# Two memory heads' scores inside the inversion, two weight splits and two PSUM banks moved, in the first mixer of a hybrid-layer chain

## The chip, the cores and the metric

One core of one Trainium2 chip. The metric is the device time of the whole kernel in microseconds (us); lower is better. 0.3% of it, 3.8 us, is about what a measurement of this kernel can tell from no change.

## The reference

The kernel computes a first hybrid layer (pooling and forgetting attention over 272 tokens of width 1024) and then two layers with feed-forward blocks of width 2816. The change lies in the mixer of the first of these two layers, which adds a gated delta rule (6 heads of 128, two chunks of 128 tokens here) and an attention over 256 memory rows (4 heads of 64):

```python
h = rms_norm(x, mix_norm) @ a_w_in               # 26 columns of 128: k, q, v, q_mem, gate
qkv = silu(causal_depthwise_conv(qkv, conv_w))
t_mat = where(strict, (k_beta k^T) * decay, 0) + eye      # one per head, inverted
u, w = inv(t_mat) (v * beta), inv(t_mat) (k_beta * exp(g))
# recurrence over the chunks
v_new = u_c - w_c state
out   = q_c state + qk_c v_new
state = state * d_c + k_c^T v_new
# memory attention, 4 heads
o_m = softmax(q_mem k_mem^T / 8) v_mem
x = x + concatenate([rms_norm(o) * silu(gate), o_m]) @ w_out
```

## The kernel before

All matrices that come from weights are streamed: SyncE loads slabs of two units (a unit is one column of 8 blocks of 128x128) into a ring of 4 (`raw`), ScalarE rounds a unit into `w_hi`, VectorE writes the rest into `w_lo`, and TensorE does three products for each block, so that the sum has float32 accuracy. On ScalarE `slot(u)` is the rounding of unit u+4, on VectorE `slot(u)` is the low half of unit u+3. TensorE waits for the low half of its unit (`unit_begin`), and SyncE's next load into a slab waits for it as well. Every engine's order of work is written out by hand; engines wait on counting semaphores only.

**The input projection of the mixer** is a loop over t = 0 to 24 on each engine (`for t in range(26)` on ScalarE and VectorE, `for t in range(25)` on TensorE), one unit of `w_in_a` for each t. Beside it run, for each tile, the convolution taps on VectorE (L1383), Silu on ScalarE (L764), and in the last turns the preparation of the delta rule: TensorE's Gram products of head h at t = 17 + h (L2232), GpSimd's differences of decays, ScalarE's two Exp of them for each head (L801, L802), and VectorE's `grams(h)` at t = 18 + h (L1357, L1359), which joins both and counts `n_ready`. The Gram product of head h waits for `n_ready` of head h - 2 (for h = 3 to 5), because they share banks. At t = 13 ScalarE takes the Exp of a few columns (L788, L789). At t = 19, 21 and 23 TensorE turns two heads' values (L2244) into a side bank, and ScalarE scales them back to SBUF at t = 20, 22 and 24 (L812, `vt_done`); the second turn waits for the first `vt_done`.

**The inversion** has 7 levels in two groups of three heads. In each of the first 6 levels TensorE does, for each group, a product (L2170 on `side`) and three transposes (L2165), and then for each group a joining product (L2170 on `main`). VectorE masks between them (`first_factor` L1373, `second_factor` L1377), ScalarE copies (`copy_packed` L818, `inv_x` L825), GpSimd masks the next level's factor (L1836). The groups' factors lie in main banks 3 and 0, `product` in side banks 0 and 2, `turn_bank` in side banks 3 and 1.

**The recurrence** (`each`, L2293) follows. With E1 to E6 for its six rounds of six heads, S0 to S3 for a memory head's scores (L1919), P0 to P3 for the four transposes of its probabilities (L1935), O0 to O3 for its outputs (L1961), and T for the last six transposes of the inversion (L2165), TensorE's order is:

```
S0 E1 T S1 P0 E2 E3 S2 E4 O0 P1 S3 E5 O1 P2 E6 O2 P3 O3, squares of the outputs (L2338)
```

A memory head also needs VectorE's `row_maxima` (L1042, L1058) after S, ScalarE's `exps` (L555, two instructions) after that, VectorE's `normalise` (L1066, L1068) before P, and ScalarE's `copy_pt` (L564) between P and O. E1 writes the new values that ScalarE copies (`new_values`, L830); E2 (which waits for both groups' last `second_factor`) makes the new state, E3 and E6 make outputs that VectorE copies (`by_heads`, L1486) and ScalarE squares (L836, L838), E4 prepares the second chunk's right-hand side (L1505), E5 its new values. VectorE's low halves (L986 into `w_lo`) stand between these, `slot(u0 + 24)` behind the copies of E3 and `slot(u0 + 25)` behind the last `normalise`; ScalarE's `slot(u0 + 25)` (L519) stands behind the copies of E1. `scores(MEM_A)` and `scores(MEM_A + 1)` write to side banks 0 and 3, and E1 writes to main banks 1 and 2. Then the outputs are normed and gated (L1519 to L1541, with two table loads on ScalarE, L861 and L865), and `mix_out` multiplies them by `w_out`.

Of the kernel before, what the change touches and what calls it, by code (L numbers as in the profile page):

```python
# [14 lines left out]
P = 128  # L15
# [133 lines left out]
def program(nc, dram, out):  # L149
    with ExitStack() as ctx:  # L150
# [180 lines left out]
        evac = sem("evac")  # L331
# [89 lines left out]
        def gram_bank(h):  # L421
            return (side[3], side[1], side[0])[h % 3]
# [4 lines left out]
        def product(g):  # L427
            return side[2 * g]
# [19 lines left out]
        def score_bank(a):  # L448

            return side[3] if a >= MEM_A and a % 2 else side[0]  # L450
# [51 lines left out]
        def _(act):  # L502
# [249 lines left out]
            for t in range(26):  # L752
# [46 lines left out]
                for h in {18: (0,), 19: (1, 2), 20: (3,), 21: (4, 5)}.get(t, ()):  # L799
                    act.wait_ge(diff_ready, h + 1)  # L800
                    act.activation(dec[:, h, 0, :], dec[:, h, 0, :], ACT.Exp, scale=-1.0)  # L801
                    act.activation(dec[:, h, 1, :], dec[:, h, 1, :], ACT.Exp).then_inc(decay_ready, 1)  # L802
                    if h == 3:
                        act.wait_ge(diff_ready, DH)
                        act.activation(spread[:, :, P:SEQ], spread[:, :, P:SEQ], ACT.Exp).then_inc(late_ready, 1)
                if t in (20, 22, 24):
                    j = (t - 20) // 2
                    act.wait_ge(turned_v, j + 1)
                    act.wait_ge(kv_ready, 1)
                    for i in range(4):  # L810
                        h, c = 2 * j + i // 2, i % 2
                        ins = act.activation(kqv[:, 12 + h, c * P:(c + 1) * P], side[2][:, i * P:(i + 1) * P],  # L812
                                             ACT.Copy, scale=kv_scale[:, c, h:h + 1])
                    ins.then_inc(vt_done, 1)
# [5 lines left out]
            for level in range(1, LEVELS):  # L820
                for g in range(GROUPS):
                    copy_packed(g, level)
                for g in range(GROUPS):
                    act.wait_ge(x_ready, 2 * level - 1 + g)
                    act.activation(inv_x[:, g, :, :], by_three(product(g)), ACT.Copy).then_inc(x_copied, 1)  # L825
            for g in range(GROUPS):
                copy_packed(g, LEVELS)
            def new_values(dst, j, seen):
                act.wait_ge(rec_pe, seen)
                act.activation(dst[:, 3 * j:3 * j + 3, :], rec[j][:, 0:3 * P], ACT.Copy).then_inc(rec_act, 1)  # L830
# [10 lines left out]
            exps(MEM_A)  # L841
            new_values(vn0, 0, 1)
            new_values(vn0, 1, 2)
            slot(u0 + 25)
            exps(MEM_A + 1)
            copy_pt(MEM_A)
            act.wait_ge(rec_dve, 4)
            square_outputs(0)
            exps(MEM_A + 2)
            copy_pt(MEM_A + 1)  # L850
            new_values(vn1, 0, 9)
# [123 lines left out]
        def _(dve):  # L975
# [498 lines left out]
            for level in range(1, LEVELS):  # L1474
                if level > 1:
                    for g in range(GROUPS):
                        first_factor(g, level)
                for g in range(GROUPS):
                    second_factor(g, level, turn_bank(g))
            for g in range(GROUPS):  # L1480
                first_factor(g, LEVELS)
# [7 lines left out]
            dve.wait_ge(q_decayed, 1)  # L1489
            row_maxima(MEM_A)  # L1490
            for g in range(GROUPS):
                second_factor(g, LEVELS, packed(g))
            row_maxima(MEM_A + 1)
            normalise(MEM_A)
            for j in range(2):
                by_heads(state, rec[2 + j], j, 3 + j)
            normalise(MEM_A + 1)
            for j in range(2):
                by_heads(o_a[:, :, 0:P], rec[j], j, 5 + j)
            slot(u0 + 24)  # L1500
            row_maxima(MEM_A + 2)
# [7 lines left out]
            row_maxima(MEM_A + 3)  # L1509
            take_output(om_a[:, 0, :], MEM_A + 1)  # L1510
# [346 lines left out]
        def _(pe):  # L1857
# [322 lines left out]
            for t in range(25):  # L2180
# [37 lines left out]
                if t >= 17 and t - 17 < DH:  # L2218

                    h = t - 17  # L2220
                    bank = gram_bank(h)
                    if h == 0:
                        pe.wait_ge(sums_ready, 1)
                    elif h == 1:
                        pe.wait_ge(kt_done, 1)
                    elif h == 2:
                        pe.wait_ge(sums_ready, 2)
                    else:
                        pe.wait_ge(n_ready, h - 2)
                    for i, other in enumerate((h, 6 + h)):  # L2230
                        for c in range(2):
                            ins = pe.matmul(bank[:, (2 * i + c) * P:(2 * i + c + 1) * P], kqv[:, h, chunks[c]],  # L2232
                                            kqv[:, other, chunks[c]], start=True, stop=True)
                    ins.then_inc(gram, 1)
                if t in (19, 21, 23):
# [3 lines left out]
                    if j == 0:  # L2239
                        pe.wait_ge(kt_done, 2)  # L2240
                    else:
                        pe.wait_ge(vt_done, j)
                    for i in range(4):
                        ins = pe.transpose(side[2][:, i * P:(i + 1) * P],  # L2244
# [24 lines left out]
            for level in range(1, LEVELS):  # L2269
# [8 lines left out]
                for g in range(GROUPS):  # L2278
# [3 lines left out]
                        .then_inc(joined, 1)  # L2282

# [12 lines left out]
            scores(MEM_A)  # L2296

            pe.wait_ge(evac, in_tile(25) + 1)
            each(rec[0:2], [(lambda h: d_t[:, h, 0, :], lambda h: kqv[:, 12 + h, 0:P])],
                 (((first_ready, 2 * LEVELS - 1),), ((first_ready, 2 * LEVELS),)))  # L2300
            for g in range(GROUPS):
                pe.wait_ge(f_copied, 2 * LEVELS - 1 + g)
                turn(g, lambda i: inv_f[:, i // 3, i % 3, :], packed(g))
            scores(MEM_A + 1)
# [4 lines left out]
                 (((rec_act, 1),), ((rec_act, 2),)))  # L2309

            each(rec[0:2], [(lambda h: vn0[:, h, :], lambda h: a_t[:, 2 * h, :])], ((), ()))
            scores(MEM_A + 2)
# [3 lines left out]
            outputs(MEM_A)  # L2316
            turn_probs(MEM_A + 1)
            scores(MEM_A + 3)

            each(rec[0:2], [(lambda h: d_t[:, h, 1, :], lambda h: rhs1[:, h, :])],  # L2320
                 (((rec_dve, 7),), ((rec_dve, 10),)))
            outputs(MEM_A + 1)
# [370 lines left out]
```

## Time and profile before

| | |
|---|---|
| Median of 3 runs | 1263.31 us (1261.05 to 1264.09) |
| The profiled execution: its time | 1260.43 us |
| The profiled execution: its span | 1258.4 us |
| Mean granted TensorE clock | 0.993 of full speed |
| TensorE busy | 1224.1 us, 97% of the span |
| VectorE busy | 872.0 us, 69% |
| ScalarE busy | 689.5 us, 55% |
| GpSimd busy | 97.3 us, 8% |

The span is counted from the first to the last instruction; the execution's own time is 2.0 us more, for what lies around it. A time in the rows below is in us from the start of the span. TensorE is called PE, VectorE DVE, ScalarE ACT, GpSimd POOL and SyncE SP there; "PE side L2170 x6" is a merged stretch of six pieces on a side bank (a float32 product of 128x128 shows as two). A part in square brackets is the idle time before an instruction and what ended it. Busy TensorE time is not TensorE at its peak: an instruction's time holds its latency.

### The profile page before, as it was taken

The page shows a single profiled execution, that of the slowest core. Times are in us where ns is not written, and L with a number is a line of the kernel's source. Part 1 is how long each engine was busy: PE and PEld are TensorE (multiplying, and loading weights), DVE is VectorE, ACT ScalarE, POOL GpSimd, SP SyncE. Part 2 cuts the span into 40 slices and gives each one's busy share as a digit, 9 for nine tenths or more (in the row PEclk, how much of TensorE's full clock was granted, in tenths as well). Part 3 has the DMA queues.
Part 4 walks back from the last instruction along what each step waited for, and adds up shares of the span by engine and source line. Part 5 has one row for each costly group of instructions (what it writes and reads, how often), then busy time and mean ns, then how long its engine had stood idle before and what let it go on. Part 6 is the DMA issues. An engine that isn't in the chain of part 4 may idle for free.

```text
span 1258.4 us, 25772 instructions
## 1 busy us (share of the span) xinstructions
PE 1224.1 (97%) x9976; PEld 1201.3 (95%) x9976; DVE 872.0 (69%) x1430; ACT 689.5 (55%) x1027; POOL 97.3 (8%) x106
## 2 busy tenths in 40 slices
PE   7999999999999998989999999999999999999996
PEld 6899999999999998969999999999999989999996
DVE  7576699876655888657766756866665777766653
ACT  7455466665544677455756544644444556544431
POOL 7261000000000014400000000000000010000000
PEclk9999999999999999998999999999999999999998
DMA  8434445655654444103554653555564323555621
GB/s 342 179 135 170 174 167 171 209 196 175 230 209 142 147 160 151 35 34 125 177 191 176 249 185 108 193 184 183 211 226 144 133 95 113 191 197 183 259 93 33
DMA packets 48983, 210.01 MB, mean 167 GB/s; under 512 B 3446, under 2 KB 6020, under 8 KB 44436
## 3 DMA queue, kind: packets, MB, share of 16 engines
q1 hardware_dynamic: 47424, 204.42, 46.2%
q10 hardware_dynamic: 1492, 4.68, 1.0%
q8 instruction: 44, 0.72, 0.2%
q14 instruction: 23, 0.19, 0.0%
HBM read 207.99 MB, written 1.10 MB: 166 GB/s over the span
## 4 chain that ended last, share of the span: by engine, by line
PE 92%; DVE 5%; ACT 1%; DMA 1%; issue 1%; DVEq 0%; ACTq 0%
PE main L1866 27%; PE main L1868 27%; PE main L1867 27%; DVE w_lo L986 1%; PE side L1961 1%; PE main L2170 1%; DVE cy L1383 1%; PE main L2293 1%; PE side L1935 1%; PE side L2170 1%; PE main L2445 1%; PE main L2449 1%; PE main L2447 1%; DMA spread<-delta_rows 0%; PE side L1972 0%
## 5 line engine op out<-in xcount | busy, mean ns | idle before, releaser
L519 ACT ACTIVATE w_hi<-raw 128x1024 fp32r<-128x1024 f32 (+2 forms) x364 | 404.6, 1114 | 309.3 <-PE main L1868 302.8
L1866 PE MATMUL main<-xg_hi,w_hi 128*128 128x256 f32 (+1 forms) x2000 | 566.8, 283 | 1.2 <-DVE w_lo L986 0.8
L1867 PE MATMUL main<-xg_hi,w_lo 128*128 128x256 f32 (+1 forms) x2000 | 563.6, 282 | 0.0
L1868 PE MATMUL main<-xg_lo,w_hi 128*128 128x256 f32 (+1 forms) x2000 | 563.3, 282 | 0.0
L986 DVE TENSOR_TENSOR w_lo<-raw,w_hi 128x1024 fp32r<-128x1024 f32 (+2 forms) x364 | 468.3, 1295 | 7.0 <-ACT w_hi L519 6.2
L1866 PEld LDWEIGHTS main<-xg_hi,w_hi 128*128 128x128 f32 x2000 | 378.1, 189 | 3.0 <-DVE w_lo L986 1.2
L1868 PEld LDWEIGHTS main<-xg_lo,w_hi 128*128 128x128 f32 x2000 | 378.8, 189 | 0.0
L1867 PEld LDWEIGHTS main<-xg_hi,w_lo 128*128 128x128 f32 x2000 | 376.0, 188 | 0.5
L1866 PE MATMUL main<-h_hi,w_hi 128*128 128x256 f32 x704 | 198.3, 282 | 0.0
L1868 PE MATMUL main<-h_lo,w_hi 128*128 128x256 f32 x704 | 198.3, 282 | 0.0
L1867 PE MATMUL main<-h_hi,w_lo 128*128 128x256 f32 x704 | 198.2, 282 | 0.0
L1866 PEld LDWEIGHTS main<-h_hi,w_hi 128*128 128x128 f32 x704 | 132.6, 188 | 0.0
L1867 PEld LDWEIGHTS main<-h_hi,w_lo 128*128 128x128 f32 x704 | 132.6, 188 | 0.0
L1868 PEld LDWEIGHTS main<-h_lo,w_hi 128*128 128x128 f32 x704 | 132.6, 188 | 0.0
L1108 DVE TENSOR_TENSOR hid<-main,rstd 128x256 f32<-128x256 f32 x88 | 37.3, 424 | 100.1 <-PE main L1868 100.1
L537 ACT ACTIVATE xg_hi<-x,par 128x256 fp32r<-128x256 f32 (+2 forms) x56 | 28.1, 509 | 102.7 <-DVE x L1262 91.9
L1262 DVE SCALAR_TENSOR_TENSOR x<-main,x 128x256 f32 (+1 forms) x40 | 17.0, 425 | 94.0 <-PE main L1868 94.0
L1108 DVE TENSOR_TENSOR gate_n<-main,rstd 128x256 f32<-128x256 f32 x88 | 37.3, 424 | 35.5 <-PE main L1868 34.9
L1020 DVE SCALAR_TENSOR_TENSOR xg_lo<-x,par,xg_hi 128x256 fp32r<-128x256 f32 (+2 forms) x56 | 27.2, 493 | 30.9 <-ACT xg_hi L537 30.9
L533 ACT ACTIVATE sq<-x 128x256 f32<-128x256 f32 (+2 forms) x64 | 26.1, 407 | 40.6 <-DVE x L1262 31.2
L1297 DVE TENSOR_TENSOR hid<-hid,gate_s 128x256 f32<-128x256 f32 x86 | 36.6, 426 | 7.2 <-ACT gate_s L707 0.9
L986 DVE TENSOR_TENSOR h_lo<-hid,h_hi 128x256 f32 (+1 forms) x88 | 36.9, 420 | 0.6 <-ACT h_hi L712 0.6
(420 smaller groups left out, 1421.7 us busy)
## 6 DMA issues: line engine op xcount, KB each, us to landing
raw<-in_w_gu_a SPq DMA_DIRECT2D x44, 1024.0 KB, 5.2
raw<-in_w_gu_b SPq DMA_DIRECT2D x44, 1024.0 KB, 5.2
raw<-in_w_down_a SPq DMA_DIRECT2D x16, 1408.0 KB, 5.9
raw<-in_w_down_b SPq DMA_DIRECT2D x16, 1408.0 KB, 5.9
raw<-in_w_in SPq DMA_DIRECT2D x20, 1024.0 KB, 5.3
raw<-in_w_in_a SPq DMA_DIRECT2D x13, 1024.0 KB, 5.2
raw<-in_w_up SPq DMA_DIRECT2D x4, 1024.0 KB, 5.2
raw<-in_w_out SPq DMA_DIRECT2D x4, 1024.0 KB, 5.2
```

The lines of the kernel that those rows point to most:

```text
L519: act.activation(w_hi[:, u % RING, 0:n], raw[:, s % RAW, u % 2, 0:n], ACT.Copy).then_inc(hi_ready, 1)
L533: act.activation(sq[:, c % 2, 0:n], src, ACT.Square).then_inc(sq_ready, 1)
L537: act.activation(dst, src, ACT.Copy, scale=g).then_inc(xh_ready, 1)
L986: return dve.tensor_tensor(dst, src, hi.bitcast(F32), ALU.subtract)
L1020: dve.scalar_tensor_tensor(dst, src, g, hi.bitcast(F32), ALU.mult, ALU.subtract)\
L1108: return dve.tensor_tensor(dst, main[t % 4][0:rows, c:c + n], scale, ALU.mult)
L1262: dve.scalar_tensor_tensor(xm, main[(t + m) % 4][:, 0:SEQ], alpha, xm, ALU.mult, ALU.add).then_inc(evac, 1)
L1297: dve.tensor_tensor(hid[:, t % 2, :], hid[:, t % 2, :], gate_s[:, t % 2, :], ALU.mult)\
L1866: pe.matmul(dst, a_hi, b_hi, start=first, stop=False)
L1867: pe.matmul(dst, a_lo, b_hi, start=False, stop=False)
L1868: return pe.matmul(dst, a_hi, b_lo, start=False, stop=last)
L2170: ins = pe.matmul(dst[:, i * P:(i + 1) * P], lhs(i), rhs(i), start=first, stop=True, skip_group_check=not first)
```

## The change

- TensorE: S0 (`scores(MEM_A)`) moves to the end of level 4 of the inversion and S1 to the end of level 5; both now write to main banks 1 and 2 (`rec[0]`, `rec[1]`). E1, which writes to the same banks, now waits for both heads' Exp (`exp_ready`). S2 moves between E2 and E3, O0 between E3 and E4, P1 behind E4, O1 ahead of E5.
- VectorE: the maxima of S0 move behind the second factors of level 5 and those of S1 behind those of level 6, ahead of the last `first_factor`; `normalise` of the first head stands ahead of the last `second_factor`, that of the second behind it. `slot(u0 + 24)` moves from behind the copies of E3 to behind the last maxima.
- ScalarE: `exps` of the first head moves behind the copies of level 6, that of the second behind the last `copy_packed`; `slot(u0 + 25)` moves behind `copy_pt` of the second head; `exps` of the third comes behind `copy_pt` of the first.
- Banks: the Gram products of heads 2 and 5 go to side bank 2 instead of 0, the turned values to side bank 0 instead of 2, `product` of the two groups is swapped. So the Gram product of head 2 waits for `kt_done` (ScalarE's k_dec, L796) and no longer for `sums_ready` 2 (VectorE, L1449); the first turn of values waits for `sums_ready` 2.
- ScalarE's Exp of the decays: head 0 at t = 13 (was 18), head 1 at 18, heads 2 and 3 at 19, heads 4 and 5 at 20; the Exp of `spread` (L805) follows head 5 instead of head 3, still ahead of L812 at t = 20.

```diff
         def gram_bank(h):
-            return (side[3], side[1], side[0])[h % 3]
+            return (side[3], side[1], side[2])[h % 3]
...
         def product(g):
-            return side[2 * g]
+            return side[2 - 2 * g]
...
         def score_bank(a):
+            if a in (MEM_A, MEM_A + 1):
+                return rec[a - MEM_A]
             return side[3] if a >= MEM_A and a % 2 else side[0]
...
-                for h in {18: (0,), 19: (1, 2), 20: (3,), 21: (4, 5)}.get(t, ()):
+                for h in {13: (0,), 18: (1,), 19: (2, 3), 20: (4, 5)}.get(t, ()):
...
-                    if h == 3:
+                    if h == 5:
                         act.wait_ge(diff_ready, DH)
...
-                        ins = act.activation(kqv[:, 12 + h, c * P:(c + 1) * P], side[2][:, i * P:(i + 1) * P],
+                        ins = act.activation(kqv[:, 12 + h, c * P:(c + 1) * P], side[0][:, i * P:(i + 1) * P],
...
+            exps(MEM_A)
             for g in range(GROUPS):
                 copy_packed(g, LEVELS)
+            exps(MEM_A + 1)
...
-            exps(MEM_A)
             new_values(vn0, 0, 1)
             new_values(vn0, 1, 2)
-            slot(u0 + 25)
-            exps(MEM_A + 1)
             copy_pt(MEM_A)
+            exps(MEM_A + 2)
             act.wait_ge(rec_dve, 4)
             square_outputs(0)
-            exps(MEM_A + 2)
             copy_pt(MEM_A + 1)
+            slot(u0 + 25)
             new_values(vn1, 0, 9)
...
                     second_factor(g, level, turn_bank(g))
+                if level == 5:
+                    dve.wait_ge(q_decayed, 1)
+                    row_maxima(MEM_A)
+                if level == 6:
+                    row_maxima(MEM_A + 1)
             for g in range(GROUPS):
                 first_factor(g, LEVELS)
...
-            dve.wait_ge(q_decayed, 1)
-            row_maxima(MEM_A)
+            normalise(MEM_A)
             for g in range(GROUPS):
                 second_factor(g, LEVELS, packed(g))
-            row_maxima(MEM_A + 1)
-            normalise(MEM_A)
+            normalise(MEM_A + 1)
             for j in range(2):
                 by_heads(state, rec[2 + j], j, 3 + j)
-            normalise(MEM_A + 1)
+            row_maxima(MEM_A + 2)
             for j in range(2):
                 by_heads(o_a[:, :, 0:P], rec[j], j, 5 + j)
-            slot(u0 + 24)
-            row_maxima(MEM_A + 2)
...
             row_maxima(MEM_A + 3)
+            slot(u0 + 24)
             take_output(om_a[:, 0, :], MEM_A + 1)
...
                     elif h == 2:
-                        pe.wait_ge(sums_ready, 2)
+                        pe.wait_ge(kt_done, 2)
...
                     if j == 0:
-                        pe.wait_ge(kt_done, 2)
+                        pe.wait_ge(sums_ready, 2)
...
-                        ins = pe.transpose(side[2][:, i * P:(i + 1) * P],
+                        ins = pe.transpose(side[0][:, i * P:(i + 1) * P],
...
+                if level == 4:
+                    scores(MEM_A)
+                if level == 5:
+                    pe.wait_ge(evac, in_tile(25) + 1)
+                    scores(MEM_A + 1)
...
-            scores(MEM_A)
-
-            pe.wait_ge(evac, in_tile(25) + 1)
+            pe.wait_ge(exp_ready, 2 * (MEM_A + 2))
             each(rec[0:2], [(lambda h: d_t[:, h, 0, :], lambda h: kqv[:, 12 + h, 0:P])],
...
-            scores(MEM_A + 1)
             turn_probs(MEM_A)
...
+            scores(MEM_A + 2)
             each(rec[0:2], [(lambda h: vn0[:, h, :], lambda h: a_t[:, 2 * h, :])], ((), ()))
-            scores(MEM_A + 2)
+            outputs(MEM_A)
             each(rec[2:4], [(lambda h: kqv[:, h, P:SEQ], lambda h: state[:, h, :])],
                  (((rec_dve, 1),), ((rec_dve, 2),)))
-            outputs(MEM_A)
             turn_probs(MEM_A + 1)
             scores(MEM_A + 3)
+            outputs(MEM_A + 1)
             each(rec[0:2], [(lambda h: d_t[:, h, 1, :], lambda h: rhs1[:, h, :])],
                  (((rec_dve, 7),), ((rec_dve, 10),)))
-            outputs(MEM_A + 1)
             turn_probs(MEM_A + 2)
```

## Rows read from the trace of the kernel before

**Rows 1.** The page: busy us, share of the span and instructions of each engine.

```profile
PE 1224.1 (97%) x9976; PEld 1201.3 (95%) x9976; DVE 872.0 (69%) x1430; ACT 689.5 (55%) x1027; POOL 97.3 (8%) x106
```

**Rows 2.** Waits of TensorE: total us, times, longest us.

```profile
PE side L1935 <- DVE p_a L1068: 1.7, 1, 1.7
```

**Rows 3.** Timeline of TensorE: start us, us, the two Gram products that waited.

```profile
486.94 1.16 PE L2232 MATMUL side<-kqv 128*128 128x128 f32 x8 [2.75 <-DVE cols L1449]
...
493.66 1.16 PE L2232 MATMUL side<-kqv 128*128 128x128 f32 x8 [2.28 <-DVE a_t L1359]
```

**Rows 4.** Timeline of ScalarE, projection turns 18 to 20.

```profile
490.62 1.28 ACT L801 ACT_TABLE_LOAD   x1
...
495.66 0.40 ACT L801 ACTIVATE dec<-dec 128x256 f32<-128x256 f32 x1
495.96 0.40 ACT L802 ACTIVATE dec<-dec 128x256 f32<-128x256 f32 x1
496.27 0.83 ACT L805 ACTIVATE spread<-spread 128x768 f32<-128x768 f32 x1
497.01 1.11 ACT L812 ACTIVATE kqv<-side,cols 128x128 f32<-128x128 f32 x4
```

**Rows 5.** Timeline of VectorE: its last work before grams(0).

```profile
490.06 0.17 DVE L1457 TENSOR_TENSOR cols<-cols 128x12 f32<-128x12 f32 x1
```

**Rows 6.** The chain of waits, TensorE at projection turn 21: start us, us.

```profile
497.67 0.89 PE side L2232 x8
498.56 0.44 PE side L2244 x4
```

**Rows 7.** The chain of waits, level 6 of the inversion.

```profile
533.10 0.73 PE side L2170 x6
...
535.16 1.59 PE main L2170 x12
```

**Rows 8.** The chain of waits, recurrence: S0, E1, T, S1, P0, E2 with E3.

```profile
536.74 1.06 PE side L1919 x4
537.80 1.54 PE main L2293 x12
539.34 0.65 PE main L2165 x6
539.99 1.07 PE side L1919 x4
...
542.75 0.66 PE side L1935 x4
543.41 2.68 PE main L2293 x24
```

**Rows 9.** Timeline of VectorE: level 6 to 7, a maximum, splits, last copy.

```profile
535.20 0.56 DVE L1377 TENSOR_TENSOR d_t<-side,triangles 128x384 f32<-128x384 f32 x1 [0.44 <-PE side L2165]
...
536.78 0.56 DVE L1373 TENSOR_TENSOR d_t<-main,triangles 128x384 f32<-128x384 f32 x1 [0.36 <-PE main L2170]
537.91 0.69 DVE L1042 TENSOR_REDUCE small<-side 128x2 f32<-128x512 f32 x1 [0.57 <-PE side L1919]
...
546.92 1.22 DVE L986 TENSOR_TENSOR w_lo<-raw,w_hi 128x1024 fp32r<-128x1024 f32 x1
...
557.18 0.56 DVE L1486 COPY o_a<-main 128x384 f32<-128x384 f32 x1 [0.42 <-PE main L2293]
```

**Rows 10.** Timeline of ScalarE: last copy of the inversion, first Exp, squares, last probabilities.

```profile
537.37 0.49 ACT L818 ACTIVATE inv_f<-main 128x384 f32<-128x384 f32 x1 [0.43 <-DVE d_t L1373]
538.84 0.47 ACT L555 ACTIVATE p_a<-side,small 128x256 f32<-128x256 f32 x1 [0.97 <-DVE small L1058]
...
539.65 0.20 ACT L555 ACTIVATION_READ_ACCUMULATOR p_a<-side,small 128x1 f32 x1
...
557.77 0.84 ACT L838 ACTIVATE rhs<-o_a 128x768 f32<-128x768 f32 x1 [2.67 <-DVE o_a L1486]
558.77 0.60 ACT L564 ACTIVATE pt_a<-side 128x512 f32<-128x512 f32 x1 [0.16 <-PE side L1935]
```

**Rows 11.** Timeline of SyncE, from 530 on: start us, us, five slabs.

```profile
548.31 46.16 SPq L468 DMA_DIRECT2D raw<-in_w_gu_a  x5
```

**Rows 12.** Windows: busy us of PE, PEld, DVE, ACT, POOL (instructions), granted clock, DMA.

```profile
490.00:495.00 5.00, 2.72 (x23) 2.51 (x22) 2.56 (x8) 4.79 (x10) 0.00 (x0) 1.00 0.58 210
...
564.00:565.00 1.00, 0.38 (x2) 0.09 (x2) 0.51 (x2) 1.00 (x1) 0.00 (x0) 0.79 0.00 0
...
565.00:566.00 1.00, 0.63 (x3) 0.63 (x4) 0.91 (x2) 0.99 (x3) 0.00 (x0) 0.50 0.00 0
...
574.00:575.00 1.00, 1.00 (x7) 1.00 (x7) 0.00 (x0) 0.00 (x0) 0.00 (x0) 0.59 0.00 0
```

## The prediction

> **What bounds the kernel now.** The page comes first: TensorE is busy for 97% of the span, and no other engine is over 69% [rows 1]. So a change can win only where TensorE stands still, or by giving it less to do, and this one gives it the same products. The list of TensorE's waits, with the timeline beside it, shows where it stands still near the change: 2.75 and 2.28 us ahead of two Gram products of the projection [rows 3], and 1.7 us ahead of P0 [rows 2]. That is 6.7 us in all, about the most that the change could win, against 3.8 us (0.3%) that a measurement of this kernel can tell from no change. The timelines then give each wait's neighbours. The sum is made against the profiled execution's own 1260.43 us (its span plus 2.0 us around it), which lies 2.9 us under the median of 1263.31; I add the sum to the median.
>
> **Projection, Gram product of head 2.** It waited 2.75 us for VectorE's sums and started at 486.94 [rows 3]. Now it waits only for k_dec, long written, and runs inside that stall. But the turn of values behind it takes over the same wait, so unit 20 starts only after that turn. Saved: one Gram group, 0.89 us [rows 6]; with the turn's own cold start I count 0.9.
>
> **Gram product of head 3.** It started at 493.66, after VectorE's grams(0) [rows 3], and grams(0) waited for ScalarE's Exp of head 0, which stood behind a table load of 1.28 us at 490.62 [rows 4]. With head 0's Exp at t = 13 (two more instructions of some 0.36 us each in a turn where ScalarE then waits for VectorE's taps: free; without that cover 0.7 us), grams(0) can start when its engine gets there, at 490.2 [rows 5], and end 0.95 later (it ended at 493.6 from a start at 492.65). The Gram product starts near 491.2, some 2.5 us earlier.
>
> **What is late next.** The second turn of values, behind the Gram product of head 4, waits for the first L812. ScalarE reaches L812 at 497.01, behind the table load of 490.62, four heads' Exp, two splits and the 0.83 us of L805 [rows 4]; the table load itself follows the last Silu, which waits for VectorE's taps and which the change does not move. In the new order five heads' Exp stand between the table load and L812 instead of four: one pair, 0.61 us start to start (495.66 to 496.27 [rows 4]). So L812 ends at 498.12 + 0.61 = 498.73 and TensorE's turn, which began at 498.56 before [rows 6], begins at 498.8 and cold (0.1 more). Both gains above end in a wait there of 2.7 us. **Projection: +0.3 us.** From there on TensorE is the bound again.
>
> **Scores in the inversion.** A score takes 1.06 us, and the products behind it 1.54 instead of 1.34 (half of 2.68 for 24 pieces) [rows 8]: 0.2 us for the change between 64-row and 128-row weights, so 1.26 for each. Does a level have a gap that takes them in? A level lasts 3.64 us (533.10 to 536.74 [rows 7, 8]; six are alike); its 30 pieces of 0.111 us are 3.34 us. The 0.30 left lie ahead of the second joining product (which waits for VectorE's mask, 535.20 to 535.76 [rows 9]; 1.59 instead of 1.34 [rows 7]) and ahead of the transposes (0.73 instead of 0.67). S0 and S1 are put behind the second joining product, where TensorE does not wait. They fill at most the 0.06, so levels 5 and 6 start 1.26 us later each: **+2.5 us.** If they fit in the gaps after all it would be 2 x 0.30 less, the low end; the high end is 2 x 1.26 with nothing filled. The maxima of head 0 on VectorE (0.69 + 0.17, some 0.8 start to start [rows 9]) lie beside S1 and cost nothing; without S1 there they would hold the next masks by 0.7.
>
> A rule of the Trainium skill (TensorE: Matmul & The Clock Gate, "The mechanism") says that a weight load overlaps matmuls in flight only when its row group differs. By it 128-row loads would never overlap, a score would cost nothing at its edges, and the sum would be 0.4 lower. The trace has 24 pieces in 2.68 us with their loads overlapped, so I keep the 0.2.
>
> **E1's new wait.** In the times of before: the maxima of head 1 now stand ahead of the last `first_factor`. VectorE ends `second_factor` at 535.76, the maxima hold it to 536.48, and its two masks end at 537.52 instead of 537.34 (0.56 each [rows 9]). ScalarE's copy of the second group (0.49 [rows 10]) ends at 538.05, and only then come the Exp of head 1. A head's Exp take 1.01 us from 538.84 to 539.85 [rows 10], so they end at 538.96. E1 needs 0.04 for the semaphore, 0.27 for a cold start (1.16 instead of 0.89 [rows 3, 6]) and 1.34: it ends at 540.6. T takes 0.65, to 541.3. Behind T VectorE makes the last two `second_factor` (to 542.0, its `normalise` of head 0 being done), while TensorE does P0 (0.6). E2 starts its products at 542.0 + 0.3 = 542.35. Before, they started at 543.41 [rows 8]. From the end of level 6 at 536.74 this is 5.6 us instead of 6.7: **-1.06 us.** The 1.7 us wait, S0 and S1 are gone from here, and a wait of 2.6 us for the Exp with one of 0.4 for the factors has come.
>
> **Order of the recurrence.** The products are the same. One switch from 64-row pieces back to 128-row ones is saved, since O1 follows S3: E1 to E6 gain 0.1 to 0.2. Each new neighbour has its cover: S2 covers the state copies, S3 covers `copy_pt` of head 1, P2 (0.45) covers ScalarE's copy of E5's first half, by 0.1 us only. **-0.1.**
>
> **The splits.** VectorE's `slot(u0 + 24)` took 1.22 us at 546.92 [rows 9], but the list of waits has none of TensorE's between 543.41 and 558.7, so it cost nothing, and moving it wins nothing. It is now next to `slot(u0 + 25)`, in front of the copies of E6. By my count VectorE leaves the second at 0.2 us after E6's end instead of before it, and the last copy (0.56 at 557.18 [rows 9]) ends 0.5 late; squares (0.84) and `copy_pt` (0.60) follow in turn on ScalarE [rows 10], and O3 waits for them. ScalarE had 0.16 idle in between: **+0.35.** ScalarE's own `slot(u0 + 25)` (1.0 us) goes to a place where it waits for E5. Issues past which things move: SyncE's load of a slab of `w_gu_a2` waits for `slot(u0 + 24)` and goes out some 7 us after its 548.31 [rows 11], for use eight units on, 25 us later. The bank swap itself costs nothing: no two of its users are alive at once.
>
> **Sum:** 0.3 + 2.5 - 1.06 - 0.1 + 0.35 = +2.0 us: 1262.4 against the profiled execution, **1265.3** against the median. Bounds: with the gaps filled, 1.0 to 1.4; with ScalarE or VectorE later by one instruction at E1 and at E6, 3.5.
>
> **The rivals.**
>
> - **The projection's gain holds** (chance 0.17). If L812 is not what TensorE meets next, the 2.5 us of head 3's Gram product stay, and the sum is 2.0 - 0.3 - 2.5 = -0.8: 1262.5. For it speaks that both stalls are on TensorE's path and that what they waited for comes earlier [rows 3]; against it the order of ScalarE, in which L812 has all the Exp in front of it. With E1's wait shorter by a microsecond as well it would be 1261.5, and with the gaps filled 1260.9. To get over 0.3% faster another microsecond and a half would have to come from somewhere; chance 0.08 for all such.
> - **E1 does not feel the wait** (0.1): if the Exp of head 1 were done before the last masks, E1 would run behind level 6 and E2 at 540.9, 1.4 earlier: 1263.8. Against it stands the order on both engines.
> - **Slower: the clock falls in the recurrence** (0.08). TensorE now stands still for 2.6 us ahead of E1, and again 0.4 us ahead of E2. If the granted clock goes to 1.2 GHz there, as it did at 564.8, where it read 0.50 to 574.9 [rows 12], some 10 us at half speed cost up to 5 us of products that are on the path: 1270.3. It would decide if a stall were longer than any that the trace shows at full clock. Against it: the stall of 2.28 us, 4.4 us behind one of 2.75, left the clock at 1.00 [rows 3, 12], and the new one is no longer.
> - **The splits' place** (0.07): if VectorE is later still at E6 (each further microsecond goes one to one into O3), +3.5 to +4.5: 1267 to 1268.
>
> **How the numbers follow.** The forecast has 0.5, with a range of its own from 1264 to 1267. The range of 1260.5 to 1268.5 takes in the first, second and last rivals and the spread of the medians (3 us between three runs); it leaves out the clock's fall and the wins of over 0.3%. Faster by over 0.3% (under 1259.5): 0.08. Slower by over 0.3% (over 1267.1): the clock 0.08, the splits' place and the forecast's upper end 0.09, together 0.17. Within 0.3%: 0.75.
>
> **What would show each step.** The Gram product of head 2 starts near 484.2 and that of head 3 near 491.2; the turn of values behind head 4 shows a wait of over 2 us for ScalarE's L812. Levels 5 and 6 last 4.9 us instead of 3.64. E1 waits 2 to 3 us for L555. P0 no longer waits; E2 does, for L1377. The last copy of E6 starts behind a split. The prediction is wrong if L812 ends before 497.5, if a level takes in a score for less than 0.8 us, or if the clock reads 0.50 between 535 and 560.

## The result, and the profile after

| | before | after |
|---|---|---|
| Median | 1263.29 us (1260.76 to 1264.09, 7 runs) | 1267.84 us (1266.24 to 1268.36, 7 runs) |
| The profiled execution | 1260.43 us, span 1258.4, clock 0.993 | 1268.03 us, span 1266.0, clock 0.988 |
| Ratio | | 1.0035, 95% interval 1.0025 to 1.0045 |

The changed kernel is slower by 0.35%, 4.5 us. The forecast was +2.0 us (1265.3) with 1264 to 1267 for its own range, inside a wider range of 1260.5 to 1268.5. In the runs below, one execution of the kernel before and one of experiment 12 took 1712 and 1714 us at a mean clock of 0.65; the ratios leave them out. The page, first part: TensorE has the same 9976 products and 6.8 us more of busy time for them (1224.1 in [rows 1]).

```profile
PE 1230.9 (97%) x9976; PEld 1207.3 (95%) x9976; DVE 871.5 (69%) x1430; ACT 689.5 (54%) x1027; POOL 97.7 (8%) x106
```

TensorE's timeline in the projection: the turn of values at t = 19, Gram product of head 3, the turn at t = 21.

```profile
488.74 0.63 PE L2249 MATMUL side<-const,kqv 128*128 128x128 f32 x4 [1.95 <-DVE cols L1452]
492.84 1.16 PE L2237 MATMUL side<-kqv 128*128 128x128 f32 x8 [0.63 <-DVE a_t L1362]
...
500.58 0.63 PE L2249 MATMUL side<-const,kqv 128*128 128x128 f32 x4 [2.84 <-ACT kqv L814]
...
505.40 1.05 PE L2237 MATMUL side<-kqv 128*128 128x128 f32 x8
```

And in the recurrence: E1, T, P0, the new state (E2), and O3 at its end.

```profile
545.07 2.54 PE L2303 MATMUL main<-kqv,d_t 128*128 128x128 f32 x12 [2.22 <-ACT p_a L557]
547.40 1.49 PE L2170 MATMUL main<-const,inv_f 128*128 128x128 f32 x6
548.68 0.73 PE L1940 MATMUL side<-const,p_a 128*128 128x128 f32 x4
549.54 1.60 PE L2303 MATMUL main<-vn,k_dec 128*128 128x128 f32 x12
...
566.09 1.08 PE L1966 MATMUL side<-pt_a,mem_v 128*64 128x256 f32 x4 [1.06 <-ACT pt_a L566]
```

The stalls stand where the prediction put them. What it did not have is E1's own time: 2.54 us for 12 products, where the six heads took 1.54 in [rows 8]. The windows of after say why (busy us of PE, PEld, DVE, ACT and POOL, then the granted clock):

```profile
500.00:505.00 5.00, 4.42 (x25) 4.45 (x26) 0.00 (x0) 1.38 (x3) 0.00 (x0) 0.66 0.26 108
545.00:550.00 5.00, 4.80 (x26) 4.56 (x27) 1.59 (x5) 1.55 (x4) 0.00 (x0) 0.66 0.00 0
568.00:570.00 2.00, 2.00 (x18) 2.00 (x17) 0.00 (x0) 1.57 (x2) 0.00 (x0) 0.85 0.00 0
570.00:580.00 10.00, 7.61 (x30) 6.21 (x31) 7.69 (x14) 5.05 (x8) 0.00 (x0) 0.50 0.00 0
580.00:584.00 4.00, 4.00 (x25) 4.00 (x24) 1.97 (x5) 1.06 (x3) 0.00 (x0) 0.62 0.00 0
```

Of before, the same kind of windows, with 1.00 behind both stalls of [rows 3]:

```profile
500.00:505.00 5.00, 5.00 (x45) 5.00 (x44) 2.96 (x7) 2.38 (x6) 2.13 (x1) 1.00 0.56 178
545.00:550.00 5.00, 5.00 (x33) 3.83 (x33) 4.93 (x14) 1.96 (x6) 0.00 (x0) 1.00 0.05 10
564.00:576.00 12.00, 10.29 (x48) 9.19 (x49) 8.56 (x15) 4.93 (x8) 0.00 (x0) 0.57 0.00 0
```

The clock goes to 1.2 GHz behind the stall at 497.8 to 500.6, and again behind the one at 542.9 to 545.1; and the low stretch at the end of the mixer is longer: by the windows 13.6 us at half speed (2 x (0.15 x 2 + 0.50 x 10 + 0.38 x 4)) against 10.3 (2 x 0.43 x 12). There is a fourth low stretch, far ahead of the change, in the kernel's first part:

```profile
160.00:165.00 5.00, 5.00 (x32) 5.00 (x32) 4.11 (x6) 4.69 (x5) 0.00 (x0) 0.68 0.55 211
```

The profiled execution of before had a clock of 1.00 there. The experiments show that this one comes in executions of either kernel.

### The profile page after: what moved, and what is told of

The parts are those of the page before. It is cut to its first block, busy times and chain, and to the rows that moved or that the text cites. A ratio compares the mean times of both kernels' runs of the same rounds, so it can differ in the third digit from the quotient of the medians.

```text
span 1266.0 us, 25773 instructions
## 1 busy us (share of the span) xinstructions
PE 1230.9 (97%) x9976; PEld 1207.3 (95%) x9976; DVE 871.5 (69%) x1430; ACT 689.5 (54%) x1027; POOL 97.7 (8%) x106
## 4 chain that ended last, share of the span: by engine, by line
PE 87%; DVE 8%; ACT 2%; issue 1%; DMA 1%; DVEq 0%; ACTq 0%
PE main L1871 26%; PE main L1873 26%; PE main L1872 26%; DVE w_lo L989 2%; DVE cy L1386 2%; PE side L1966 1%; PE main L2175 1%; PE main L2303 1%; PE side L2175 1%; PE side L1940 1%; PE main L2452 1%; PE main L2456 1%; PE main L2454 1%; DMA spread<-delta_rows 0%; DVE cx L1111 0%
```

## The experiments

Theory A: the schedule got 2 us worse, as forecast, and the rest of the loss is TensorE's clock, which falls behind the two stalls. Rival B: the schedule itself costs 4.5 us (the stall ahead of E1, or the splits' new place). Rival C: both halves of the change lose on their own, and the losses add up. Each kernel was timed beside the kernel before, whose median was 1263.28, 1263.21, 1263.19 and 1263.15 us in the four sets.

**1. The projection's part alone.** The kernel before with the new order of the decays' Exp and the new banks; inversion and recurrence as they were.

```diff
-            return (side[3], side[1], side[0])[h % 3]
+            return (side[3], side[1], side[2])[h % 3]
...
-                for h in {18: (0,), 19: (1, 2), 20: (3,), 21: (4, 5)}.get(t, ()):
+                for h in {13: (0,), 18: (1,), 19: (2, 3), 20: (4, 5)}.get(t, ()):
```

> The kernel before with only the projection's part of the change (Exp of head 0 at t = 13, the others one turn earlier, the bank swap). Theory A (the order of ScalarE makes a stall ahead of the turn of values, and TensorE's clock then falls behind it): a wait of about 2.8 us for L812, the clock at 0.50 for some 3 us behind it, and +2.0 us in all, of which 0.3 is the later L812 and 1.7 the clock. Rival B (the loss is all in the inversion and the recurrence): 0 to +0.3 us, clock at 1.00 in the projection.

Measured: 1263.82 us (11 runs), ratio 1.0005 [0.9996, 1.0014]. The wait for L812 is there, and behind it the fall:

```profile
500.00:505.00 5.00, 4.52 (x26) 4.55 (x27) 0.00 (x0) 1.28 (x3) 0.00 (x0) 0.66 0.27 110
```

Yet the time is half a microsecond over before, not the 2 that theory A expected. Either the fall costs less than it seems, or before pays for one as well. Experiment 9 takes this up.

**2. The inversion's and the recurrence's part alone.** The changed kernel with the lines of experiment 1 undone.

> The changed kernel with the projection's part undone (decays and banks as before), so the scores in levels 4 and 5, E1's wait, the moved splits and the new order alone. Theory A: 2 x 1.26 in the levels, -1.06 at E1 to E2, +0.25 for order and tail, so +1.7 without the clock, and +1.2 to +2 more where the clock falls behind E1's wait: +3 us. Rival B: +4.5 us, all of what the change costs. Rival C (the clock has no part): +1.7.

Measured: 1263.63 us (11 runs), ratio 1.0009 [1.0000, 1.0019]. The wait ahead of E1 was 2.2 us as in after, but E1 took 1.60 us: the clock did not fall behind it in that profile. That is less than any of the three expected (+3, +4.5, +1.7). The halves lose 0.5 and 0.4 us by the medians (at most 1.8 and 2.4 by the intervals), the whole 4.5: the losses do not add up as rival C has it, and rival B's cost of 4.5 us in the schedule of the inversion and the recurrence is not there. The halves meet in something.

**3. Heads 4 and 5 behind the values.** Their Exp, and with them that of `spread`, go back to t = 21, so L814 has only three heads' Exp ahead of it behind the table load.

```diff
-                for h in {13: (0,), 18: (1,), 19: (2, 3), 20: (4, 5)}.get(t, ()):
+                for h in {13: (0,), 18: (1,), 19: (2, 3), 21: (4, 5)}.get(t, ()):
```

> The changed kernel with the Exp of decay heads 4 and 5, and so that of spread, behind the first L812 (t = 21 instead of 20). Theory A: L812 ends some 1.9 us earlier than in the changed kernel, the wait of 2.8 us shrinks to about 1 us and the clock stays at 1.00 there: 3 to 4 us less than the changed kernel, about +0.5 us against before. If the clock has no part: 2 us less, +2.5 against before. If the wait is not on the path: no change, +4.5.

Measured: 1263.28 us (11 runs), ratio 1.0002 [0.9993, 1.0011]: 4.6 us under the changed kernel. The wait for L814 went from 2.8 to 0.9 us, and the clock stayed at 1.00 through 500 to 505. It fell behind E1's wait instead:

```profile
540.00:545.00 5.00, 4.83 (x27) 4.64 (x28) 1.70 (x5) 1.54 (x5) 0.00 (x0) 0.66 0.00 0
```

**4 to 6. The stalls filled.** The test that changes the clock and not the order: products that nothing reads, on a bank that is free there, ahead of the wait. The engine then works where it stood, and what it waits for comes no earlier. Ten ahead of the wait for L814, nine ahead of E1's:

```diff
+                        if j == 1:
+                            idle = bank_of(in_tile(t + 1))
+                            for _ in range(10):
+                                pe.matmul(idle[:, 0:P], ident, ident, start=True, stop=True)
                         pe.wait_ge(vt_done, j)
...
+            for _ in range(9):
+                pe.matmul(product(0)[:, 0:P], ident, ident, start=True, stop=True)
             pe.wait_ge(exp_ready, 2 * (MEM_A + 2))
```

Both:

> The changed kernel with products that nobody reads put in TensorE's two stalls: ten float32 products of 128x128 (2.2 us) ahead of the wait for L812, nine (2.0 us) ahead of E1's wait. The waits' ends do not move. If the clock falls because TensorE stands still there, it stays at 1.00 through both places, the unit behind the first takes 2.85 us and E1 1.6, and the time is 2.5 to 3 us under the changed kernel (+1.5 to +2 against before). If the clock falls for another reason or costs nothing: +4.5, as the changed kernel.

The first alone:

> The changed kernel with the ten unread products ahead of the wait for L812 alone, none ahead of E1. Theory A: the clock's fall in the projection goes (1.7 us), the one behind E1's wait may stay (1.2 us): +2 to +3 us against before. If the stall ahead of E1 were what costs: +4.5. If filling one were as good as filling both: 0.

The second alone:

> The changed kernel with 9 unread products in the stall ahead of E1 alone; with them in both stalls it took 1263.26, with them in the projection's stall alone 1263.84, with none 1266.9 and 1267.84. Theory A, that each stall costs what its own fall of the clock costs (1.7 us in the projection, 1.0 to 1.2 ahead of E1): 1266 to 1266.7, the fall at 500 to 506 us there in the profile, none at 545 to 550. Theory B, that the fall ahead of E1 hangs on the one in the projection, and filling one stall is enough: 1263.3 to 1264. The wait for the second head's Exp stays at 2.2 us by its end: the four matrices are written no earlier.

Measured, each in 11 runs, all with the changed kernel's instructions and more:

| unread products | us | ratio to before |
|---|---|---|
| none (7 runs, and 6 of experiment 7) | 1267.84, 1266.9 | 1.0035, 1.0028 |
| ahead of E1 | 1265.16 | 1.0016 [1.0007, 1.0025] |
| ahead of the values' turn | 1263.84 | 1.0006 [0.9997, 1.0015] |
| both | 1263.26 | 0.9999 [0.9990, 1.0008] |

TensorE gets 19 products more to do and the kernel is 3.6 to 4.6 us faster; its lowest run, 1262.43, is also 2.6 us under the lowest of the 13 of the changed kernel. That the clock costs something here is shown; it costs more than the 2.5 to 3 us expected. The turn of values did not start any earlier for them: it waits as long as ScalarE makes it, only with less idle time in front.

```profile
495.95 2.40 PE L2250 MATMUL main<-const 128*128 128x128 f32 x20
...
498.88 0.66 PE L2253 MATMUL side<-const,kqv 128*128 128x128 f32 x4 [0.53 <-ACT kqv L814]
```

The two do not add up as separate falls: alone they save 4.0 and 2.7 us of 4.6 against 1267.84 (3.1 and 1.7 of 3.6 against 1266.9), so both expectations for one stall filled were missed. With the projection's filled, +0.6 is nearer to the rival's 0 than to theory A's +2 to +3; with E1's filled, 1265.16 lies between theory B (1263.3 to 1264) and theory A (1266 to 1266.7), though the profile is the one that A described. Experiments 1, 2, 3 and 8 say the same: each has only one of the two stalls and comes within 0.6 us of before by its median, though in three of their profiles (1, 3 and 8) the clock fell behind it. The profile with E1's stall alone filled has the fall at 500 to 504 and none at 545; the one with the projection's stall filled has none at either, though E1's wait is still 2.2 us. So whether E1's stall brings the clock down varies from one execution to the next. Whether it does so less often when it did not fall in the projection can't be said from one profile a kernel: experiment 3 has the fall behind E1's stall alone. How the two are tied stays open.

**7. The changed kernel again**, for a second profile.

> The changed kernel itself, again, on the chip of the runs beside it. Theory A (two stalls of ordering, +2.0 us, and the clock falling behind each, +2.5 us): +4.5 us, clock near 0.988. If the first measurement of it held an accident of its chip: +2 us.

Measured: 1266.9 us (6 runs), ratio 1.0028 [1.0016, 1.0040]; the same four stretches of low clock, at 160 to 164, 502 to 505, 546 to 550 and 570 to 580. The last is shorter than in the first profile, 10.2 us at half speed against 13.6, so its length too varies between executions of one kernel.

**8. The scores one level earlier.** S0 and S1 in levels 3 and 4, with their maxima and Exp, so that E1 finds the second head's Exp done.

```diff
-                if level == 5:
+                if level == 4:
                     dve.wait_ge(q_decayed, 1)
                     row_maxima(MEM_A)
...
-                if level == 4:
+                if level == 3:
                     scores(MEM_A)
```

> The changed kernel with both scores, their maxima and the first head's Exp one level earlier (S0 in level 3, S1 in level 4, Exp of head 1 ahead of the last copies). Theory A: E1's wait of 2.2 us goes and leaves only the waits for the last masks, E2 starts 1.4 us earlier relative to the inversion, and no clock falls there (1.2 us more): 1.4 to 2.6 us under the changed kernel, +2 to +3 against before. If E1's wait is covered by what follows: as the changed kernel.

Measured: 1263.61 us (11 runs), ratio 1.0004 [0.9995, 1.0012]. E1's wait for L557 is gone from the list, no fall behind it; the one at 500 to 503 stays. The time is 3.3 us under the changed kernel's 1266.9, where theory A expected 1.4 to 2.6.

**9. Before, with its stalls filled.** Ten unread products ahead of Gram head 2's wait, eight ahead of head 3's, six ahead of P0's.

```diff
+                        for _ in range(10):
+                            pe.matmul(bank_of(in_tile(t + 1))[:, 0:P], ident, ident, start=True, stop=True)
                         pe.wait_ge(sums_ready, 2)
```

> The kernel before with products that nothing reads in its stalls: 10 ahead of Gram head 2's wait, 8 ahead of Gram head 3's, 6 ahead of P0's. Theory A, that a fall of the clock follows a stall of TensorE of over 2 us in some executions of the kernel before too (its median is 2.9 us above the profiled execution, which had none there): 1 to 2.5 us under the kernel before, toward 1260.5 to 1262. Theory B, that before's median comes from something else and only the change's longer stalls bring the clock down: the same as before, 1263.2, ratio 0.9995 to 1.0005. In both, the profile shows Gram head 2 and P0 begin where they began before, to 0.1 us.

Measured: 1260.39 us (10 runs), ratio 0.9976 [0.9966, 0.9985]: 2.8 us faster than before, with 24 products more. Against experiment 10's profile Gram head 3 (495.34 and 495.28), S0 (538.42 and 538.35) and the new state (545.09 and 545.02) begin where they did. So before too seems to pay for its stalls, in its common executions: their mean clock is mostly 0.988 to 0.990, that of this kernel 0.991 to 0.994. No profile has caught such a fall (those of before, of experiment 10 and of experiment 2, which has the same two stalls in the projection, read 1.00 behind them); that it comes behind the stalls at 484 to 502 or behind P0's is inferred from the times. The one profile of this kernel, its slowest run at 1262.48, has the fall at 160 and is no faster than experiment 10's, 1261.98, which has it too.

**10. Before, a second profile.**

> The kernel before itself, for a second profile. If its median of 1263.3 against 1260.4 in the first profile is the clock's doing, this profile has a fall of the clock that the first has not, ahead of 480 us or behind the stalls at 494 to 502 us, worth 1.5 to 3 us, with a mean granted clock near 0.990; if it is one of the quick executions it is at 1260.4 to 1261 again, with the clock at 0.993.

Measured: 1261.98 us, clock 0.992, and one fall that the first profile has not:

```profile
160.00:165.00 5.00, 5.00 (x31) 5.00 (x31) 4.05 (x6) 4.64 (x5) 0.00 (x0) 0.66 0.61 211
```

From there everything runs 1.6 us later: Gram head 2 starts at 488.57, not at 486.94. The median of 1263.2 is another 1.2 above this one.

**11. Rearranged.** Experiments 3 and 8 together, each score put between its level's two joining products, and VectorE's `slot(u0 + 24)` back behind the copies of E3.

```diff
+                    if g == 1 and level == 3:
+                        scores(MEM_A)
+                    if g == 1 and level == 4:
+                        pe.wait_ge(evac, in_tile(25) + 1)
+                        scores(MEM_A + 1)
...
                 by_heads(o_a[:, :, 0:P], rec[j], j, 5 + j)
+            slot(u0 + 24)
...
             row_maxima(MEM_A + 3)
-            slot(u0 + 24)
```

> The changed kernel with L812 ahead of the Exp of heads 4 and 5, the scores one level earlier and between the two joining products of their level instead of behind them, and VectorE's slot(u0 + 24) back behind the copies of E3. From values_first (no loss against before): 1.4 us less at E1, 0.25 us less for each score, 0.35 less ahead of O3, and the clock at 1.00 up to the squares: 2.2 to 3.5 us under before. Rival (the stalls that go are taken up by the next wait): no better than values_first, 0 against before.

Measured: **1259.6 us** (1258.4 to 1261.23, 6 runs), ratio 0.9969 [0.9957, 0.9981]: faster than before by 0.3%, and than the changed kernel by 8.2 us (7.3 against experiment 7), with the same instructions. It is just beyond the 2.2 to 3.5 us expected. Not all of this is the clock's: 3.7 us lie between it and the changed kernel with both stalls filled (1263.26), whose clock did not fall in this part either, and O3 begins 4.0 us earlier than there (559.12 less 1.6 for the fall at 160, against 561.48). Its list of TensorE's waits in this part (total us, times, longest us) has nothing of 2 us left:

```profile
PE side L2250 <- DVE cols L1453: 1.9, 1, 1.9
PE side L1967 <- ACT pt_a L566: 1.1, 1, 1.1
...
PE side L2250 <- ACT kqv L814: 0.9, 1, 0.9
```

and of the low stretches of the clock it has the ones at 160 and at 564 to 574 only. A level with a score lasts 4.6 us instead of 4.83, since the score now fills the wait for VectorE's mask.

**12. Rearranged, with the rest filled.** Unread products in five places that are left: 8 ahead of the turn at t = 19, 4 at t = 21, and 4, 3 and 4 from O3 to the gated output.

> The rearranged kernel (combined, 1259.6) with unread products in the stalls that it has left: 8 ahead of the turn at t=19, 4 ahead of the turn at t=21, 4 ahead of the third output product, 3 ahead of the output state's and 4 ahead of the gated output's products. Theory A, that the low stretch at 562 to 574 us comes from the stalls and the turns ahead of it: the stretch is gone or shorter, and the time is 1.5 to 3 us under combined, 1256.5 to 1258. Theory B, that the low stretch follows the squares and column sums, which the products do not touch: the stretch stays and the time is within 0.6 us of combined, 1259.0 to 1260.2.

Measured: 1260.54 us median of 12 runs, ratio 0.9978 [0.9969, 0.9987], 0.9 above experiment 11 and just above what B expected. The low stretch stays, and by the windows it is longer, 13.6 us at half speed against 10.2:

```profile
565.00:570.00 5.00, 5.00 (x22) 4.55 (x22) 3.44 (x6) 2.05 (x4) 0.00 (x0) 0.50 0.00 0
```

Theory A's part of it falls. Filling is no cure in itself: it pays where it keeps a fall away, and here none was kept away.

## Why the prediction was right or wrong

**The ledger.** The changed kernel with both stalls filled shows the new schedule with the clock at 1.00 up to 564, as in the first profile of before: so up to O3 the two can be laid side by side without the clock.

| starts at (us) | before | both stalls filled | after |
|---|---|---|---|
| Gram head 4 | 497.51 | 495.06 | 496.68 |
| Gram head 5 | 501.67 | 502.21 | 505.40 |
| O3 | 559.42 | 561.48 | 566.09 |
| first product of the output projection | 572.24 | 574.47 | 579.43 |
| first turn of probabilities in the next layer's mixer | 1008.01 | 1011.06 | 1015.65 |
| span | 1258.4 | 1260.4 | 1266.0 |

The schedule costs 2.1 us up to O3: the sum was +2.0. That the span is 2.0 longer as well is chance. Behind the output projection's first product the clock stays low for 4.4 us in the filled kernel and for 2.6 in before, and by the mixer of the next layer it is 3.0 us late. There it gains 1.0 us: VectorE's `normalise` and GpSimd's products start within 0.4 us of each other, and in before and after VectorE's pair takes 2.23 and 2.24 us and TensorE waits for it, in the filled kernel 0.62 and it does not. Nine of the 14 profiles have this wait and five (experiments 2, 12 and 4 to 6) do not, and the change does not touch this place.

```profile
1010.57 2.23 DVE L1068 TENSOR_SCALAR s_b<-s_b,small 128x256 f32<-128x256 f32 x2
...
1012.86 0.66 PE L1935 MATMUL side<-const,s_b 128*128 128x128 f32 x4 [1.08 <-DVE s_b L1068]
...
1013.59 0.62 DVE L1071 TENSOR_SCALAR s_b<-s_b,small 128x256 f32<-128x256 f32 x2
```

The first two lines are of before, the third of the kernel with both stalls filled. From this kernel to after it is 5.0 us at the output projection's first product: 1.62 from the fall at 160 (485.74 against 484.12 at Gram head 2), 1.57 from that behind the values' turn (505.40 less 1.62, against 502.21), 1.42 from that behind E1 (from E1's start to that of the new state 4.47 instead of 3.05), and 0.37 from squares that run partly at half speed (3.15 us for 24, against 2.78). Then 0.4 come back, since after's clock stays low for only 3.6 us behind that product, and the wait in the next layer's mixer adds 1.0: 5.6 us of span.

**Step by step.**

- **Gram head 2 early, turn of values late: right.** Predicted start 484.2, measured 484.12 with no fall ahead; the turn behind it took over the wait, 1.95 us.
- **Gram head 3: right.** Predicted 491.2; 491.22, and 492.84 in after, 1.62 of it from the fall at 160.
- **What is late next: right.** ScalarE's L814 was forecast to end at 498.73, with a wait of 2.7; in the filled kernel it ends at 498.83 and the turn begins at 498.88, and in after the wait is 2.84. The projection loses 0.54 us (Gram head 5 in the ledger), forecast 0.3. Rival "the projection's gain holds" is out.
- **Scores in the inversion: right.** Two levels of 4.83 us each (531.60 to 536.43 and on to 541.27 in the chain), forecast 4.90. The score takes 1.06 and the next product 0.86 instead of 0.73. The Trainium skill's rule (TensorE: Matmul & The Clock Gate, "The mechanism") gave nothing at the edges; the trace has 0.13 us behind the score in each level (0.86 less 0.73), so the measurement decides against it.

```profile
531.60 1.58 PE main L2175 x12
533.18 1.06 PE main L1924 x4
534.24 0.86 PE side L2175 x6
...
536.43 1.59 PE main L2175 x12
```

- **E1's wait: right in mechanism and nearly in size.** It is 2.22 us. The prediction says 2.6, but its own times give 2.26 (538.96 and 0.04, less 536.74). ScalarE's order is the one predicted: the copies end, then two Exp, then E1. In the filled kernel the new state starts 5.25 us behind the end of level 6 (544.93 less 539.68), forecast 5.6, before 6.67: a gain of 1.42 instead of 1.06. Rival "E1 does not feel the wait" is out.

```profile
543.15 0.95 ACT L820 ACTIVATE inv_f<-main 128x384 f32<-128x384 f32 x2 [0.78 <-DVE d_t L1376]
544.00 0.47 ACT L557 ACTIVATE p_a<-main,small 128x256 f32<-128x256 f32 x1
544.36 0.20 ACT L557 ACTIVATION_READ_ACCUMULATOR p_a<-main,small 128x1 f32 x1
544.45 0.47 ACT L557 ACTIVATE p_a<-main,small 128x256 f32<-128x256 f32 x1
```

- **Order, splits and tail: right in kind, short by 0.3.** Up to O3 the terms are 0.54 + 2.38 - 1.42 + 0.54, against 0.3 + 2.5 - 1.06 + 0.25, order and tail taken together. The total of 2.06 (rounding aside) came out at the forecast's 2.0 because the misses of single terms cancel. The last copies on VectorE stand behind the second split, and O3 waits 1.06 us:

```profile
562.53 1.22 DVE L989 TENSOR_TENSOR w_lo<-raw,w_hi 128x1024 fp32r<-128x1024 f32 x1
563.66 1.01 DVE L1494 COPY o_a<-main 128x384 f32<-128x384 f32 x2
```

- **The clock: wrong, and this is the step that failed.** It stood under the rivals at 0.08, as one fall of 10 us in the recurrence for 5 us. What came was two short ones of about 3.4 us each for 1.4 to 1.6, the first of them in the projection, where the prediction had a stall of 2.7 us in its own working and did not ask what it does to the clock. By the prediction's own sign of being wrong, a clock of 0.50 between 535 and 560, it was wrong: after reads 0.50 from 546 to 548. The argument against it was one profile of before, in which stalls of 2.75 and 2.28 us left the clock at 1.00 [rows 3, 12]. Experiment 9 makes that likely to be an exception: filled, the kernel before is 2.8 us faster in the median. The sign that was there to be read was the profiled execution's place, 2.9 us under the median: the text took that as an offset to be added. 1.6 of it is the fall at 160, which experiment 10 caught; that the rest are falls behind stalls is inferred.

So the changed kernel lost three times: 2.1 us by the schedule, some 0.8 by a longer low stretch at the mixer's end (together 2.9 by the medians of the two filled kernels, 1263.26 less 1260.39), and the remaining 1.7 because the falls of the clock ahead of it cost 4.6 us (1267.84 less 1263.26) where those of before cost 2.8. The longer stretch was no term of the sum either: all four profiles with the recurrence of before have 10.2 us at half speed there, seven of the eight with the changed one have 13.6 or more.

The forecast was 2.5 us short, and "slower by over 0.3%", at 0.17, is what happened. That the range held the time is luck: its upper part stood for the splits' place, and the clock's fall was left out of it.

## What to carry to other kernels

When an order is rewritten, add up not only the idle time of the bounding engine but how it is cut: here two waits of over 2 us cost 1.4 to 1.6 us more each through the clock in the profile, and an order of the same work in which none is over 2 us turned +4.5 us into -3.6, about half of it through the clock and half through less idle time. Before arguing from one profile that a stall leaves the clock alone, look at where that execution lies among the runs and at their mean clocks. Unread products ahead of a wait are a cheap test for what a stall costs through the clock, since the waiting instruction starts when it did. Before taking a span that fits the sum as proof, compare start times along the way: here 2.0 was 3.0 less 1.0.

## What the runs showed of the hardware

- TensorE stood still for 2.84 and 2.22 us, and behind each the granted clock was at its lower level (1.2 GHz) for about 3.4 us (2 x 0.34 x 5, by the windows) before it rose again. The 2.84 us had a fall behind them in all five profiles that have this wait (after, experiments 1, 7, 8, and the one with E1's stall alone filled). The 2.2 us ahead of E1 had one in three profiles (after, experiments 3 and 7) and none in two (experiment 2, and the one with the values' stall alone filled). The waits of 2.75 and 2.28 us of the kernel before had none in three profiles (before, experiments 2 and 10), and the 1.95 us ahead of the turn at t = 19 had none in any.
- The same program has executions with and without a fall of the clock at 160 us, 1.6 us apart (1260.43 and 1261.98 for before), with no instruction moved ahead of it.
- The stretch of low clock at the end of the mixer (it begins between 562 and 570 us) lasts from 10.2 us (before, experiment 11) to 17 us (E1's stall alone filled), though TensorE is busy for much of it (7.6 of 10 us in after's windows), and filling five idle places around it (experiment 12) did not shorten it. What ends it is open.
- Two instructions of VectorE take 0.62 us or 2.23 us in the same place of the next layer's mixer, where GpSimd starts within 0.4 us of them; TensorE waits 1.1 us in the second case. What decides between the two is open.
